# Seven of the twelve input projections moved into the steps of the attention, with heads taken in the order of the query tiles

## What is computed

```python
z = rmsnorm(x, pre_mix_g) @ w_in          # q: 512 columns, k and v: 128 each, cq: 384, ckv: 256, kr: 32, gates: 2048
qa = rope(rmsnorm(q per head)); ka = rope(rmsnorm(k per head))      # 8 query heads, 2 key heads, width 64
ya = softmax(qa @ ka.T / 8) @ va          # a key head serves 4 query heads
qb = rmsnorm(cq) @ w_q_up                 # 8 latent heads: 64 columns plain, 32 rotated
kb, vb = rmsnorm(ckv) @ w_kv_up; the rotated 32 columns of kb come from rope(kr)
yb = softmax(qb @ kb.T / sqrt(96)) @ vb
merged = gate_a * (ya @ w_branch_a) + gate_b * (yb @ w_branch_b);  x += rmsnorm(merged @ w_o)
```

## Time and profile before

| What | us |
|---|---|
| median of three runs (3027.43 to 3029.3) | 3027.64 |
| the profiled execution, its own time | 3033.26 |
| its span in the trace | 3031.4 |
| PE busy in the span | 2844.3 |
| layer 0, from the fifth projection's end to the third score product's end | 40.5 to 84 |
| layer 0, steps 3 to 31 | 84 to 181.3 |
| layer 0, latent heads, steps 31 to 59 | 181.3 to 268.1 |
| the same three stages of layer 1 begin at | 866.7, 909.8, 1007 |

### The profile page before, as it was taken

How to read it: one execution, slowest core, us unless ns; L and a number is a source line. 1 busy time by engine, 2 the same in 40 slices (tenths; PEclk the granted TensorE clock), 3 DMA queues, 4 the chain that set the end, 5 groups by cost and what they waited for, 6 DMA issues and landing times.

```text
span 3031.4 us, 33713 instructions
## 1 busy us (share of the span) xinstructions
PE 2844.3 (94%) x12862; PEld 2326.4 (77%) x12862; DVE 1615.2 (53%) x2075; ACT 1151.1 (38%) x1758; POOL 735.0 (24%) x597
## 2 busy tenths in 40 slices
PE   7998999999988989999999976999999999999998
PEld 5676887888766768878887775878887789878886
DVE  5677446334366774463343986555533558555533
ACT  4566234222245663342223263332232337522221
POOL 2364113313123641131132262022200003112200
PEclk9999999999989999999999887999999989999999
DMA  3110332333211113223332201232332210122332
GB/s 127 35 36 29 97 98 84 98 97 96 92 63 35 42 35 96 93 84 97 98 98 97 84 14 43 84 104 95 96 103 96 90 56 1 56 88 96 96 104 90
DMA packets 75634, 236.68 MB, mean 78 GB/s; under 512 B 9776, under 2 KB 18240, under 8 KB 75488
## 3 DMA queue, kind: packets, MB, share of 16 engines
q1 hardware_dynamic: 74288, 231.31, 23.7%
q0 software_dynamic: 928, 3.27, 0.3%
q10 hardware_dynamic: 272, 0.06, 0.0%
HBM read 228.31 MB, written 2.10 MB: 76 GB/s over the span
## 4 chain that ended last, share of the span: by engine, by line
PE 83%; DVE 10%; ACT 3%; POOL 1%; issue 1%; DMA 1%; SPq 1%; DVEq 0%; POOLq 0%; ACTq 0%
PE bank L1739 26%; PE bank L1741 25%; PE bank L1740 25%; PE bank L2035 2%; PE bank L1899 1%; DVE S5S L1607 1%; DVE STAT L1433 1%; DMA RAWW<-weights 1%; DVE WL L1322 1%; PE bank L1941 1%; DVE S5S L1598 1%; SPq L766 1%; ACT WH L1017 1%; POOL FF L818 1%; DVE RL L1327 1%
## 5 line engine op out<-in xcount | busy, mean ns | idle before, releaser
L1322 DVE TENSOR_TENSOR WL<-RAWW,WH 128x1024 fp32r<-128x1024 f32 (+2 forms) x424 | 570.1, 1348 | 846.1 <-ACT WH L1017 846.0
L1739 PE MATMUL bank<-UH,WH 128*128 128x512 f32 (+1 forms) x1920 | 763.0, 397 | 55.2 <-DVE UL L1332 29.6
L1740 PE MATMUL bank<-UL,WH 128*128 128x512 f32 (+1 forms) x1920 | 754.9, 393 | 0.0
L1741 PE MATMUL bank<-UH,WL 128*128 128x512 f32 (+1 forms) x1920 | 754.6, 393 | 0.0
L1017 ACT ACTIVATE WH<-RAWW 128x1024 fp32r<-128x1024 f32 (+2 forms) x424 | 433.5, 1026 | 368.8 <-DMA RAWW<-weights 368.4
L1739 PEld LDWEIGHTS bank<-UH,WH 128*128 128x128 f32 (+1 forms) x1920 | 365.4, 190 | 143.8 <-issue 59.5
L1740 PEld LDWEIGHTS bank<-UL,WH 128*128 128x128 f32 (+1 forms) x1920 | 365.2, 190 | 78.2 <-issue 2.4
L1741 PEld LDWEIGHTS bank<-UH,WL 128*128 128x128 f32 (+1 forms) x1920 | 364.6, 190 | 78.3
L1739 PE MATMUL bank<-HH,WH 128*128 128x512 f32 x512 | 199.2, 389 | 0.0
L1740 PE MATMUL bank<-HL,WH 128*128 128x512 f32 x512 | 199.2, 389 | 0.0
L1741 PE MATMUL bank<-HH,WL 128*128 128x512 f32 x512 | 199.2, 389 | 0.0
(11 more groups left out here) (336 smaller groups left out, 4726.8 us busy)
## 6 DMA issues: line engine op xcount, KB each, us to landing
RAWW<-weights SPq DMA_DIRECT2D x424, 512.0 KB, 3.4
X<-x SPq DMA_DIRECT2D x8, 256.0 KB, 5.4
FF<-tables POOLq DMA_DIRECT2D x2, 1024.0 KB, 7.5
U<-S5U SPq DMA_DIRECT2D x16, 128.0 KB, 2.4
GEL<-U SPq DMA_DIRECT2D x128, 16.0 KB, 1.8
out<-FF SPq DMA_DIRECT2D x8, 256.0 KB, 2.0
S5B<-s_b POOLq DMA_DIRECT2D x1, 512.0 KB, 3.8
S5C<-s_c POOLq DMA_DIRECT2D x1, 512.0 KB, 4.4
```

What stands on the lines that cost most here:

```text
L1322: dve.tensor_tensor(slot_words(WL, c % SLOTS, size), slot_words(RAWW, c % SLOTS, size), f32(slot_words(WH, c % SLOTS, size)), ALU.subtract ...
L1739: nc.tensor.matmul(out_, w[0], x_[0], start=start, stop=False, **how)
L1740: nc.tensor.matmul(out_, w[0], x_[1], start=False, stop=False, **how)
L1741: return nc.tensor.matmul(out_, w[1], x_[0], start=False, stop=stop, **how)
```

## The change

- Five projections ahead: k, q0, v, q1, q2. Seven woven into the attention: q3, cq0, cq1, cq2, ckv0, ckv1, kr, issued in steps 2, 4, ..., 14. The list of (step, what, tile) is the new table `SCHEDULE`; a step's `issue` is the projection, `evacuate` its evacuation, `total` the matmuls that sum the squares (now in TURN for q1, q2, q3 as well), `root` and `turn_in` the factor.
- The first eight heads are taken in the order of the query tiles: head h reads tile h // 2 and key half h % 2, so step 0 needs k and q0 only, step 8 q1, step 16 q2, step 24 q3. The weight stream on the host follows the new order.
- The low parts get a step kind of their own. `turn_out` is now ACT's part alone and `turn_low` is DVE's. In the woven steps `turn_low` is one step later. For the latent heads it is in the same step, but behind `att_lo` and `att_out_lo` instead of ahead of `att_scores`.
- `latent` keeps DVE's multiply and ACT's high part. DVE's subtraction moves to `latent_low`, one step later.
- q1 to q3 are evacuated into CF and squared into RKV and RCQ, and the squares of cq and ckv go to a new tile SPARE or RKV. The waits that guard these buffers change with them.

```diff
-LAST_Q, POST_MIX, POST_FFN = 1 + QT, 4 + QT, 6 + QT
+LAST_LEAD, POST_MIX, POST_FFN = 2, 4 + QT, 6 + QT
...
         if 0 <= h < 2 * HEADS and phase == 3:
             plan.add("att_out_lo", h=h, pv=h)
+        if 1 <= m_out <= HEADS and out_phase == 1:
+            plan.add("turn_low", **rotation)
         latents(x)
...
+SCHEDULE = [
+    (0, "turn_in", "q1"), (1, "turn_rest", "q1"), (2, "turn", "q1"), (2, "issue", "q3"), (3, "total", "q2"), (3, "evacuate", "q3"),
+    (4, "turn_out", "q1"), (4, "turn_in", "q2"), (4, "issue", "cq0"), (5, "turn_low", "q1"), (5, "turn_rest", "q2"),
+    (5, "evacuate", "cq0"), (6, "turn", "q2"), (6, "issue", "cq1"), (7, "total", "q3"), (7, "evacuate", "cq1"),
+    (8, "turn_out", "q2"), (8, "turn_in", "q3"), (8, "issue", "cq2"), (9, "turn_low", "q2"), (9, "turn_rest", "q3"),
+    (9, "evacuate", "cq2"), (10, "turn", "q3"), (10, "issue", "ckv0"), (11, "total", "cq0", "cq1", "cq2"), (11, "evacuate", "ckv0"),
+    (12, "turn_out", "q3"), (12, "root", "cq"), (12, "issue", "ckv1"), (13, "turn_low", "q3"), (13, "latent", "cq0"),
+    (13, "evacuate", "ckv1"), (14, "latent_low", "cq0"), (14, "total", "ckv0", "ckv1"), (14, "latent", "cq1"), (14, "issue", "kr"),
+    (15, "latent_low", "cq1"), (15, "root", "ckv"), (15, "latent", "cq2"), (15, "evacuate", "kr"), (16, "latent_low", "cq2"),
+    (16, "turn_in", "kr"), (16, "latent", "ckv0"), (17, "latent_low", "ckv0"), (17, "turn_rest", "kr"), (17, "latent", "ckv1"),
+    (18, "latent_low", "ckv1"), (18, "turn", "kr"), (20, "turn_out", "kr"), (21, "turn_low", "kr")]
...
+    names = ["k", "q0", "v", "q1", "q2", "q3"] + [f"cq{i}" for i in range(CQT)] + [f"ckv{i}" for i in range(CKT)] + ["kr"]
...
     def first_products(x, mm):
...
+        name = names[x]
+        mms[name] = mm
+        evacuate(name)
+        if name == "q0":
+            rotate("turn_in", "k")
+            rotate("turn_rest", "k")
+        elif name == "v":
+            rotate("turn", "k")
+            rotate("turn_in", "q0")
+            rotate("turn_rest", "q0")
+            rotate("turn_out", "k")
+            rotate("turn_low", "k")
+        elif name == "q1":
+            rotate("turn", "q0")
+            plan.add("gqa_v", "b vh", x=ev["v"].x, j=ev["v"].j)
+            rotate("turn_out", "q0")
+            rotate("turn_low", "q0")
+        elif name == "q2":
+            total("q1")
...
     def latents(x):
...
+        for at_, do, *what in SCHEDULE:
+            if at_ == x:
+                dict(issue=issue, evacuate=evacuate, total=total, root=root).get(do, lambda *w: None)(*what)
+                if do[:4] == "turn":
+                    rotate(do, *what)
+                elif do[:6] == "latent":
+                    latent(do, *what)
+
+    linear(plan, [job(name) for name in names[:5]], dict(norm=norm, evac=first_products))
...
-                a = h // QT * HD
-                return QH, QL, slice(a, a + HD), h % QT
+                a = h % 2 * HD
+                return QH, QL, slice(a, a + HD), h // 2
...
                     dve.tensor_tensor(CF[:, k, :], CF[:, k, :], (RCQ if st.what == "cq" else RKV)[:], ALU.mult).then_inc(c_n.sem, 1)
+                elif kind == "latent_low":
+                    k, gain = small_input(l, st)
                     dve.wait_ge(c_h.sem, c_h.after(l, st.cn))
...
-                elif kind == "turn_out":
+                elif kind == "turn_low":
                     dve.wait_ge(rdone.sem, rdone.after(l, st.rot))
                     dve.wait_ge(rot_h.sem, rot_h.after(l, st.rot))
...
-                    if st.h < QT and st.t == 0:
-                        pe.wait_ge(rot_l.sem, rot_l.after(l, 1 + st.h))
+                    if st.h < HEADS and st.h % 2 == 0 and st.t == 0:
+                        pe.wait_ge(rot_l.sem, rot_l.after(l, 1 + st.h // 2))
```

More of the change, by code:

```diff
@@ L233, in plan_layer @@
     norm = plan.add("norm", NORM, gain=0, version=0)
[L234 to L237, removed]
-    def first_products(x, mm):
[L240 to L275, removed]
-    def latents(x):
[L279 to L297, removed]
@@ L299, in plan_layer, with kind_of, job @@
[L299 to L300 removed]
+    names = ["k", "q0", "v", "q1", "q2", "q3"] + [f"cq{i}" for i in range(CQT)] + [f"ckv{i}" for i in range(CKT)] + ["kr"]
+    ev, mms, sums = {}, {}, {}
+    def kind_of(name):
+        return name.rstrip("0123456789"), int(name[-1]) if name[-1].isdigit() else 0
+    def job(name):
+        return dict(kt=[DT], cols=QK if name == "kr" else P, rhs="u")
@@ new lines, in issue, with evacuate @@
+    def issue(name):
+        mm = mms[name] = plan.add("mm", "c j", first=False, ring=2, **job(name))
+        mm.bank = mm.j % 2
+        plan.cut_to(done_of(mm) + 1)
+    def evacuate(name):
+        what, i = kind_of(name)
+        mm = mms[name]
+        take = {"q": "s rot", "k": "s rot", "v": "", "cq": "s", "ckv": "s", "kr": "rot"}[what]
+        ev[name] = plan.add("evac_" + what, take, what=what, i=i, x=len(ev), j=mm.j, bank=mm.bank, done=mm.c,
+                            group=1 + len(ev) if name in ("k", "q0") else None)
@@ new lines, in rotate, with total @@
+    def rotate(kind, name):
+        what, i = kind_of(name)
+        take = "b" if kind == "turn" else "g qk" if kind == "turn_in" and what != "kr" else ""
+        plan.add(kind, take, what=what, i=i, x=ev[name].x, rot=ev[name].rot, s=ev[name].s, j=ev[name].j, h=0,
+                 rows=QK if what == "kr" else P, group=ev[name].group)
+    def total(*group):
+        for name in group:
+            what, i = kind_of(name)
+            first = name == group[0]
+            st = plan.add("turn_sum", "b" if first else "", what=what, i=i, s=ev[name].s, first=first, last_s=name == group[-1])
+            b = st.b if first else b
+            st.b = b
+        sums[kind_of(name)[0]] = st
@@ new lines, in latent, with root @@
+    def latent(kind, name):
+        what, i = kind_of(name)
+        if kind == "latent":
+            cn[name] = plan.add(kind, "cn", what=what, i=i, g=sums[what].g).cn
+        else:
+            plan.add(kind, what=what, i=i, cn=cn[name])
+    cn = {}
+    def root(what):
+        st = plan.add("rc_" + what, "g", s=sums[what].s)
+        sums[what].g = st.g
+    def first_products(x, mm):
+        name = names[x]
[17 more added lines that the diff above has]
+            total("q1")
@@ L1841, in step @@
                     pe.wait_ge(sq.sem, sq.after(l, st.s))
-                    nc.tensor.matmul(TURN[:], ONES, latent_square(st), start=st.first, stop=st.half).then_inc(summed.sem, 1)
-                    if st.half:
+                    nc.tensor.matmul(TURN[:], ONES_HEAD if st.what == "q" else ONES, own_square(st), start=st.first, stop=st.last_s
+                                     ).then_inc(summed.sem, 1)
+                    if st.last_s:
                         pe.sem_inc(turn.sem, 1)
```

52 lines of the change are left out of this document (33 added, 19 removed).

## The result

The kernel after takes 3058.84 us (median of 4 runs, 3055.22 to 3062.35). The kernel before, run beside it on the same chip, took 3028.47. The ratio is 1.0096, 95% interval 1.0081 to 1.0111: slower by 30.4 us. The forecast was slower by 15.4, 3043 us, with a range of 3022 to 3058, and the result lies 0.8 us above that range. The sign was right, the size was half of what came.

A forecast was written before the change was run, and what follows sets the result against it. PE was taken as the bound: its unchanged work plus idle time and low clock. Per layer 9.4 + 5.0 - 4.1 - 2.6 = 7.7 us lost, 15.4 for both, so 3027.6 + 15.4 = 3043 us, range 3022 to 3058.

The forecast's parts named there:

- Part 2: Steps 3 to 31: 2.6 us a layer gained, with about 5.2 us of waits in steps 15 to 23.
- The waits foreseen in step 6: Step 6: PE waits about 0.85 us for `att_lo` and 1.15 for RL, behind DVE's low part of q1.
- the one in step 14: Step 14: the ckv sum waits about 1.2 us for ckv1's evacuation and square.
- Part 1: The lead and steps 0 to 2: 4.1 us a layer gained, bounds 2.4 and 7.
- Part 3: Latent heads: late MQL stalls PE 2.0 to 2.1 us a head; 9.4 us a layer lost, bounds 7.7 and 14.7.
- Part 4: Clock in the latent heads: falls after half of seven stalls, 1.5 us each, 5 us a layer lost.
- The fall at 143.5: Steps 3 to 31: the clock's fall at 143.5, which costs 2.8 us at 0.51, probably goes.
- a fall of the clock after nearly every stall: Rival, latent heads: the clock falls after nearly every stall, 25.4 us lost, 3053 us; chance 13%.

The follow-up runs named there:

- experiment 2: Kernel after, with only the wait ahead of cq2's square loosened to the sum of q3's square, three tiles back: 3049.99 us, 1.0068 to the kernel before.
- Experiment 5: Kernel with MQL's old place and the loosened cq2 wait (3025.3 us), latent tiles' work spread over steps to 25: 3018.48 us, 0.9965 to the kernel before.
- Experiments 1 and 4: 1: kernel after, MQL of the latent heads back ahead of the reduction, 3036.07 us. 4: kernel before, only that MQL put late, 3054.52 us.

## Why the prediction missed by half

**The failed step** is the last sentence of its sum: "The new waits on `summed` and `turned_in` guard buffers whose readers are done a step earlier, at no cost." The reader of RKV is done in step 7, but the wait is not for the reader. It is for the sum one tile back, which the new table makes in step 11. The forecast looked at the buffer and not at the number in the wait. Shown by experiment 2: with the wait for the right tile the kernel is 8.9 us faster, of the 15 that were missing.

**Part 2, DVE's list.** The forecast gave DVE 12.1 us of work in steps 15 to 18. The time from one reduction to the fourth behind it after was 15.0 us (137.16 to 152.20). CL 1.59, CF 1.76 and twice CL 1.15 in place of 0.75, 0.68, 0.75 and 0.75 are 2.7 of the 2.9 more. So the waits came to 7.4 us and not 5.2: a second term of the sum that was mis-sized. The forecast knew the effect for RL (0.68 or 1.74) and took it into part 3, where POOL is known to be at work, but not here. The Trainium skill, "SBUF — State Buffer", section "SBUF: two separate sides", describes an exclusive lock between DVE, when it has two SBUF inputs, and POOL, held for the whole instruction. The trace agrees: the blocked ones end 0.54 to 0.55 us after POOL's end. The new place of CL helps it along: before, all five CL of a layer take 0.75 us, and after, four of the five in layer 0 take 1.15 to 1.59, because they now stand right behind PGL, while POOL scales the exponentials of the same step. Experiment 5 shows that the crowding costs time. What of that cost is the meeting with POOL and what the mere number of instructions was not taken apart. Of the 8.5 us a layer that part 2 missed, the wait for the square sum is 4.4, and 2.2 are the waits behind DVE's longer list. The rest, about 2, is within the estimate of the work moved and the clock, and stays open. The waits foreseen in step 6 came (1.03 and 0.96 us against 0.85 and 1.15), the one in step 14 was 0.56 and not 1.2.

**Part 1** was right in kind. The first score product started at 51.65 (forecast 51.9), and PE idled 0.78 + 2.86 = 3.6 us in the steps 0 to 2 (forecast 3.6). Not foreseen was 1.41 us for VL ahead of the first score product. The gain was 3.1 us and not 4.1, inside its bounds.

**Part 3** held. The stalls were 1.76 and 2.01 in turn (forecast 2.0 to 2.1), and 2.45 for the first head, which has QL and not YBL ahead of it. In layer 0 the low clock within the heads lasted 6.8 us, worth 3.4, so the stalls net of what they gave back cost 12.9 - 3.4 = 9.5 us (forecast 9.4). In layer 1 it is 11.5 - 1.7 = 9.8. Experiments 1 and 4 show the cause from both sides, 22.8 and 25.7 us for both layers.

**Part 4** was too high. The clock fell once in the seven counted heads of each layer, 6.8 and 3.4 us long, worth 3.4 and 1.7 us at most, against 5 forecast. Its price of 1.5 us for 3.4 us at half the clock should have been 1.7 by its own reason. The fall at 143.5 did go, as forecast.

So the sum was 2 x (3.1 gained, 5.9 and 12.2 lost) = 30.0 us, beside 30.4 measured, where 12.2 is the mean of the heads of both layers. Of the rivals, a fall of the clock after nearly every stall would have given 3053, nearest to the result, for a reason that the traces refute. No rival held a wait that is stricter than its buffer needs.

## What to carry to other kernels

- A wait is priced by the event that it names, not by the buffer that it guards. After a reordering, look up for each "n tiles back" where that tile's event now stands in the list, and what is queued behind the wait.
- When a cut or a copy is given a place of its own, it belongs ahead of the instructions in the same engine's list that wait for the engine that needs it. Here DVE's reduction waits for PE, and PE's next product waits for MQL. One moved line in a large change cost 22.8 us, and the rest of the change, with the wait repaired, gained 3.5.
- Woven work is spread by the load of the engine that serves it. In steps 15 to 18 here DVE had 2.9 to 4.5 us of work and PE 1.8, and PE waited. With the two repairs, a wider table and q3 in step 0 the change gave 0.88% (3003.5 us) where it had cost 0.96%.

## What the runs showed of the hardware

- A DVE instruction on two operands in memory that meets POOL's tensor_tensor was 1.15 to 1.76 us long in place of 0.68 to 0.75, and POOL's own grew from 1.04 to 1.48 and from 1.29 to 1.72. In layer 0 of the kernel after, each CL, CF, RL, QL (of q) and MQL that began while such an instruction of POOL was running ended 0.53 to 0.57 us after POOL's end. Where DVE's began a little ahead it kept its 0.68, and POOL's grew (in the kernel before, 225.23 and 225.26 us: 0.68, and 1.80 for MKL).
- PE's clock fell less often than the size of the idle stretches suggested. With the stall of 2.45 us that ended at 187.66 it went to 0.50 (1.2 GHz) for 6.8 us, with six stalls of 1.76 and 2.01 us in the same layer it stayed at 2.4 GHz. In layer 1 it fell in the heads after the stall of 2.01 at 1059.35 and not after that of 2.45 at 1031.62. Behind the last head's stall of 2.23 us it fell for 3.4 us in layer 0 (284.57) and not in layer 1 (1127.16). The size of one stretch does not decide it.
